# Selections over 136 candidate sums and one-pass weighted one-hot rows in a one-core decoder trunk

## The reference

```python
sc = jnp.einsum('bshcd,hcnd->bshcn', q, sub_keys)      # 8 heads, 2 halves, 128 keys each
top_s, top_i = lax.top_k(sc, 16)
cand_s = top_s[..., 0, :, None] + top_s[..., 1, None, :]             # 16 x 16 sums
cand_i = top_i[..., 0, :, None] * 128 + top_i[..., 1, None, :]
best_s, best_pos = lax.top_k(cand_s.reshape(..., 256), 16)
expert_idx = jnp.take_along_axis(cand_i, best_pos, axis=-1)
gates = jax.nn.softmax(best_s, axis=-1)
act = jax.nn.gelu(einsum('ced,cd->ce', expert_u[expert_idx], x))     # 128 experts a token
out = einsum('ce,ced->cd', gates * act, expert_v[expert_idx])
```

## Time and profile before

| what | us |
|---|---|
| runs: median of 3 (lowest to highest) | 2029.2 (2025.63 to 2031.04) |
| profiled execution: span from first to last instruction | 2043.0 |
| PE busy | 1942.4 |
| DVE busy | 1190.6 |
| POOL busy | 870.7 |
| ACT busy | 445.9 |

### The profile page before, as it was taken

The page is one execution under the profiler, slowest core; times in us unless marked ns, Lnnn a source line. Parts: engine busy times, 40 slices in busy tenths (PEclk is TensorE's granted clock), DMA queues, the critical chain, the costliest instruction groups (busy, mean ns, idle before and its releaser), DMA issues.

```text
span 2043.0 us, 23964 instructions
## 1 busy us (share of the span) xinstructions
PE 1942.4 (95%) x9007; PEld 1255.0 (61%) x9007; DVE 1190.6 (58%) x2972; ACT 445.9 (22%) x1045; POOL 870.7 (43%) x785
## 2 busy tenths in 40 slices
PE   8999999999889999999998888999999989999998
PEld 7688886956775887885676765444445543333332
DVE  1022101003896888788899989887867775444321
ACT  2233211111202454121211354000013321101112
POOL 0000000000684423445658355844557776666543
PEclk9999999999999999999999568999999999999999
DMA  7543454434999877999899677999999999999997
GB/s 237 147 121 109 148 155 144 145 103 136 373 388 349 280 255 239 369 386 388 331 359 371 221 261 243 410 409 409 409 376 348 344 334 410 409 409 409 409 389 278
DMA packets 252439, 613.48 MB, mean 300 GB/s; under 512 B 18676, under 2 KB 121124, under 8 KB 252324
## 3 DMA queue, kind: packets, MB, share of 16 engines
q0 software_dynamic: 110592, 402.70, 52.5%
q1 hardware_dynamic: 141120, 208.17, 29.7%
q10 hardware_dynamic: 612, 1.07, 0.2%
HBM read 609.77 MB, written 2.10 MB: 300 GB/s over the span
## 4 chain that ended last, share of the span: by engine, by line
PE 65%; DMA 13%; DVE 9%; POOL 7%; issue 3%; another core or an unknown queue 1%; ACT 1%; SPq 0%; POOLq 0%; DVEq 0%; ACTq 0%
PE ps L617 26%; PE ps L896 11%; PE ps L846 8%; DMA u_rows<-in_peer_u_dram,idx 7%; PE ps L632 7%; POOL u_rows L576 5%; DVE u_rows L1391 4%; PE ps L886 3%; PE ps L659 3%; POOL v_rows L590 2%; DMA wring<-in_w_in_dram 2%; DMA v_rows<-in_peer_v_dram,idx_turned 2%; PE ps L646 1%; PE ps L685 1%
## 5 line engine op out<-in xcount | busy, mean ns | idle before, releaser
L576 POOL DMA_INDIRECT u_rows<-in_peer_u_dram,idx x512 | 584.5, 1142 | 977.1 <-DVE idx L1378 508.2
L1391 DVE CUSTOM_DVE_ANT_0 u_rows<-u_rows,xn 128x1024 f32<-128x1024 f32 x512 | 621.3, 1217 | 177.8 <-DMA u_rows<-in_peer_u_dram,idx 165.2
L617 PE MATMUL ps<-xT,wring 128*128 128x256 f32 x2432 | 553.1, 386 | 22.3 <-DMA wring<-in_w_in_dram 10.1
L617 PEld LDWEIGHTS ps<-xT,wring 128*128 128x128 f32 x2432 | 464.0, 193 | 90.8 <-DMA wring<-in_w_in_dram 11.0
L896 PE MATMUL ps<-d_rows,gates 128*128 128x512 f32 x1024 | 456.3, 600 | 0.8 <-issue 0.8
L896 PEld LDWEIGHTS ps<-d_rows,gates 128*128 128x128 f32 x1024 | 190.7, 191 | 266.6 <-issue 266.6
L846 PE MATMUL ps<-v_rows,diag 64*64 64x512 f32 x1928 | 256.9, 633 | 18.9 <-DMA v_rows<-in_peer_v_dram,idx_turned 16.4
L590 POOL DMA_INDIRECT v_rows<-in_peer_v_dram,idx x121 | 135.4, 1119 | 131.3 <-PE ps L846 98.6
L886 PEld LDWEIGHTS ps<-hot_b,hot_a 128*128 128x128 f32 x1024 | 147.2, 230 | 55.4 <-issue 36.0
L886 PE MATMUL ps<-hot_b,hot_a 128*128 128x64 f32 x1024 | 155.0, 318 | 19.3 <-DVE hot_b L1458 11.0
L1091 ACT ACTIVATE diag<-ident,wgt 128x64 f32<-128x64 f32 x256 | 75.8, 336 | 435.6 <-PE ps L846 351.5
(11 more groups left out here) (201 smaller groups left out, 1747.0 us busy)
## 6 DMA issues: line engine op xcount, KB each, us to landing
wring<-in_w_in_dram SPq DMA_DIRECT2D x128, 512.0 KB
d_rows<-in_peer_v_dram SPq DMA_DIRECT2D x128, 512.0 KB
wring<-in_peer_w_query_dram SPq DMA_DIRECT2D x32, 512.0 KB
wring<-in_w_branch_conv_dram SPq DMA_DIRECT2D x16, 512.0 KB
wring<-in_w_branch_attn_dram SPq DMA_DIRECT2D x16, 512.0 KB
wring<-in_w_out_dram SPq DMA_DIRECT2D x16, 512.0 KB
wring<-in_xattn_wq_dram SPq DMA_DIRECT2D x16, 512.0 KB
wring<-in_xattn_wo_dram SPq DMA_DIRECT2D x16, 512.0 KB
```

The source lines that it names most:

```text
L576: pool.indirect_dma_start(out=u_rows[:, n % URING, :], out_offset=None, in_=peer_u[0], in_offset=bass.IndirectOffsetOnAxis(ap=experts_of(g ...
L617: mm = pe.matmul(bank(job)[:, 0:HN], w[:, k % 4, P * b:P * (b + 1)], act[:, k, :], start=(k == 0), stop=(k == KT - 1))
L1391: dve.tensor_tensor_reduce(out=u, in0=u, in1=(xn2 if h else xn1)[:, i, :], scale=1.0, scalar=0.0, op0=ALU.mult, op1=ALU.add, accum_out=dot ...
```

## The change

In `select`:

- `cand` holds 136 sums instead of 256: for each of the 16 first scores the sums with the 8 best second scores (positions 8a+b), then the first of the first scores with the other 8 second ones (positions 128 and up). The sums are sorted scores' sums, so the best 16 are always among these.
- Both indices are converted in one operation, the first no longer scaled by 128. `pos_ab` is split with other masks; `hot` is made for both numbers in one compare against two ramps `codes` (0 to 15, and 0 to 7 with 128 to 135) and one multiply. The scaling by 128 moves into the closing add.
- The generator yields twice less, so a selection ends one dot earlier.

In `one_hots` the compare and the multiply of `hot_b` over 8 tokens become eight `tensor_scalar` operations, one for each token, which compare a ramp of 64 with the token's expert number and multiply by its weight in one pass. Number and weight are one value per partition, read from `e2T` and `wT`. The semaphore `hot_half` is gone.

POOL makes one constant table more, so PE and DVE wait for 11 of them instead of 10, and the ramp `iota_a` counts in ones instead of in 128s.

```diff
-        cand = tiny("cand", [P, TOPK * TOPK])
+        cand = tiny("cand", [P, (TOPK + 1) * TOPK // 2])
...
-                candv = cand[:, :].rearrange("p (a b) -> p a b", a=TOPK)
-                t0 = after(dve.tensor_tensor(candv, top_v[:, 0, :].unsqueeze(2).to_broadcast([P, TOPK, TOPK]),
-                                             top_v[:, 1, :].unsqueeze(1).to_broadcast([P, TOPK, TOPK]), ALU.add))
+                near = TOPK // 2
+                pairs = cand[:, 0:TOPK * near]
+                rest_of_first = cand[:, TOPK * near:(TOPK + 1) * near]
+                sums = cand[:, 0:(TOPK + 1) * near]
+                dve.tensor_tensor(pairs.rearrange("p (a b) -> p a b", a=TOPK),
+                                  top_v[:, 0, :].unsqueeze(2).to_broadcast([P, TOPK, near]),
+                                  top_v[:, 1, 0:near].unsqueeze(1).to_broadcast([P, TOPK, near]), ALU.add)
+                t0 = after(dve.tensor_scalar(rest_of_first, top_v[:, 1, near:TOPK], top_v[:, 0, 0:1], None, ALU.add))
                 yield
-                dve.wait_ge(tk, t[0])
-                after(dve.tensor_scalar(top_f[:, 0, :], top_i[:, 0, :], float(NK), None, ALU.mult))
                 dve.wait_ge(tk, t0)
...
-                t2 = after(dve.tensor_copy(top_f[:, 1, :], top_i[:, 1, :]))
+                t2 = after(dve.tensor_copy(top_f[:, :, :], top_i[:, :, :]))
...
-                for c in range(2):
-                    t1 = after(dve.tensor_tensor(hot[:, c, :, :],
-                                                 pos_f[:, c, :].unsqueeze(2).to_broadcast([P, TOPK, TOPK]),
-                                                 iota16[:, :].unsqueeze(1).to_broadcast([P, TOPK, TOPK]),
-                                                 ALU.is_equal))
-                    yield
-                for c in range(2):
-                    dve.wait_ge(tk, t1 - 1 + c)
-                    after(dve.tensor_tensor(hot[:, c, :, :], hot[:, c, :, :],
-                                            top_f[:, c, :].unsqueeze(1).to_broadcast([P, TOPK, TOPK]), ALU.mult))
-                    yield
+                t1 = after(dve.tensor_tensor(hot[:, :, :, :],
+                                             pos_f[:, :, :].unsqueeze(3).to_broadcast([P, 2, TOPK, TOPK]),
+                                             codes[:, :, :].unsqueeze(2).to_broadcast([P, 2, TOPK, TOPK]),
+                                             ALU.is_equal))
+                yield
+                dve.wait_ge(tk, t1)
+                t1 = after(dve.tensor_tensor(hot[:, :, :, :], hot[:, :, :, :],
+                                             top_f[:, :, :].unsqueeze(2).to_broadcast([P, 2, TOPK, TOPK]), ALU.mult))
+                yield
...
-                dve.tensor_tensor(experts_of(g), to[:, 0, :], to[:, 1, :], ALU.add).then_inc(idx_rdy, 1)
+                dve.scalar_tensor_tensor(out=experts_of(g), in0=to[:, 0, :], scalar=float(NK), in1=to[:, 1, :],
+                                         op0=ALU.mult, op1=ALU.add).then_inc(idx_rdy, 1)
...
-                dve.tensor_tensor(hot_b[:, ch % 2, :, :],
-                                  e2T[:, i, o:o + 8].unsqueeze(2).to_broadcast([P, 8, 64]),
-                                  iota_b[:, 64 * hf:64 * (hf + 1)].unsqueeze(1).to_broadcast([P, 8, 64]),
-                                  ALU.is_equal).then_inc(hot_half, 1)
-                dve.wait_ge(hot_half, ch + 1)
-                dve.tensor_tensor(hot_b[:, ch % 2, :, :], hot_b[:, ch % 2, :, :],
-                                  wT[:, i, o:o + 8].unsqueeze(2).to_broadcast([P, 8, 64]),
-                                  ALU.mult).then_inc(hot_rdy, 1)
+                for t in range(8):
+                    last = dve.tensor_scalar(hot_b[:, ch % 2, t, :], iota_b[:, 64 * hf:64 * (hf + 1)],
+                                             e2T[:, i, o + t:o + t + 1], wT[:, i, o + t:o + t + 1],
+                                             ALU.is_equal, ALU.mult)
+                last.then_inc(hot_rdy, 1)
```

More of the change, by code:

```diff
@@ L313, in build_trunk @@
         eps_c = tiny("eps_c", [P, 1])
-        iota16 = tiny("iota16", [P, TOPK])
+        codes = tiny("codes", [P, 2, TOPK])
         xmax = tiny("xmax", [P, TT, XH])
@@ L398, in build_trunk @@
         t_out = sem("t_out")
-        hot_half = sem("hot_half")
         hot_rdy = sem("hot_rdy")
@@ L542, in _ @@
         def _(pool):
+            flat = hot[:, :, :, :].rearrange("p c a b -> p (c a b)")
             pool.memset(ident[:, :], 0.0).then_inc(consts, 1)
-            pool.memset(cand[:, 0:P], -1.0).then_inc(consts, 1)
-            pool.memset(cand[:, P:2 * P], 0.0).then_inc(consts, 1)
+            pool.memset(flat[:, 0:P], -1.0).then_inc(consts, 1)
+            pool.memset(flat[:, P:2 * P], 0.0).then_inc(consts, 1)
             pool.memset(eps_c[:, :], EPS).then_inc(consts, 1)
@@ L549, in _ @@
                                pattern=[[-1, P]], channel_multiplier=1).then_inc(consts, 1)
-            pool.affine_select(out=ntri[:, :], in_=cand[:, 0:P], compare_op=ALU.is_ge, fill=0.0, base=0,
+            pool.affine_select(out=ntri[:, :], in_=flat[:, 0:P], compare_op=ALU.is_ge, fill=0.0, base=0,
                                pattern=[[-1, P]], channel_multiplier=1).then_inc(consts, 1)
-            pool.affine_select(out=nmask_r[:, :], in_=cand[:, P:2 * P], compare_op=ALU.is_gt, fill=-1.0e30, base=0,
+            pool.affine_select(out=nmask_r[:, :], in_=flat[:, P:2 * P], compare_op=ALU.is_gt, fill=-1.0e30, base=0,
                                pattern=[[1, P]], channel_multiplier=-1).then_inc(consts, 1)
-            pool.tensor_copy(nones_r[:, :], cand[:, 0:P]).then_inc(consts, 1)
-            pool.iota(iota16[:, :], pattern=[[1, TOPK]], base=0, channel_multiplier=0,
+            pool.tensor_copy(nones_r[:, :], flat[:, 0:P]).then_inc(consts, 1)
+            pool.iota(codes[:, 0, :], pattern=[[1, TOPK]], base=0, channel_multiplier=0,
                       allow_small_or_imprecise_dtypes=True).then_inc(consts, 1)
+            pool.iota(codes[:, 1, :].rearrange("p (a b) -> p a b", a=2), pattern=[[P, 2], [1, TOPK // 2]], base=0,
+                      channel_multiplier=0, allow_small_or_imprecise_dtypes=True).then_inc(consts, 1)
             pool.wait_ge(consts, 5)
@@ L564, in _ @@
                               allow_small_or_imprecise_dtypes=True).then_inc(iotas, 1)
-                    pool.iota(iota_a[:, :], pattern=[[NK, NK]], base=0, channel_multiplier=0,
+                    pool.iota(iota_a[:, :], pattern=[[1, NK]], base=0, channel_multiplier=0,
                               allow_small_or_imprecise_dtypes=True).then_inc(iotas, 1)
@@ L597, in _ @@
         def _(pe):
-            pe.wait_ge(consts, 10)
+            pe.wait_ge(consts, 11)
             def transposes(job, tiles):
@@ L1336, in select @@
                     dve.wait_ge(gate_rdy, g - GRING + 1)
-                t1 = after(dve.max(best[:, r, 0:8], cand[:, :]))
+                t1 = after(dve.max(best[:, r, 0:8], sums))
                 yield
                 dve.wait_ge(tk, t[1])
-                t2 = after(dve.tensor_copy(top_f[:, 1, :], top_i[:, 1, :]))
+                t2 = after(dve.tensor_copy(top_f[:, :, :], top_i[:, :, :]))
                 dve.wait_ge(tk, t1)
-                t1 = after(dve.max_index(pos[:, 0:8], best[:, r, 0:8], cand[:, :]))
+                t1 = after(dve.max_index(pos[:, 0:8], best[:, r, 0:8], sums))
                 yield
                 dve.wait_ge(tk, t1)
-                t1 = after(dve.match_replace(cand[:, :], best[:, r, 0:8], cand[:, :], LOWEST))
+                t1 = after(dve.match_replace(sums, best[:, r, 0:8], sums, LOWEST))
                 yield
                 dve.wait_ge(tk, t1)
-                t1 = after(dve.max(best[:, r, 8:16], cand[:, :]))
+                t1 = after(dve.max(best[:, r, 8:16], sums))
                 yield
                 dve.wait_ge(tk, t1)
-                t1 = after(dve.max_index(pos[:, 8:16], best[:, r, 8:16], cand[:, :]))
+                t1 = after(dve.max_index(pos[:, 8:16], best[:, r, 8:16], sums))
                 dve.tensor_scalar(neg_best[:, r:r + 1], best[:, r, 0:1], -1.0, None, ALU.mult).then_inc(best_rdy, 1)
@@ L1354, in select @@
                 dve.wait_ge(tk, t1)
-                after(dve.tensor_scalar(pos_ab[:, 0, :], pos[:, :], 4, None, ALU.logical_shift_right))
-                t1 = after(dve.tensor_scalar(pos_ab[:, 1, :], pos[:, :], TOPK - 1, None, ALU.bitwise_and))
+                after(dve.tensor_scalar(pos_ab[:, 0, :], pos[:, :], 3, TOPK - 1, ALU.logical_shift_right,
+                                        ALU.bitwise_and))
+                t1 = after(dve.tensor_scalar(pos_ab[:, 1, :], pos[:, :], TOPK * near + near - 1, None,
+                                             ALU.bitwise_and))
                 yield
@@ L1489, in _ @@
                 dense_layers(unit)
-            dve.wait_ge(consts, 10)
+            dve.wait_ge(consts, 11)
             for g in range(2):
```

## The result

The change makes the kernel slower: 2039.88 us, median of 6 runs (2035.09 to 2046.23), against 2028.95 us (2023.14 to 2031.21) for the kernel before beside it. The ratio is 1.0058, with a 95% interval of 1.0038 to 1.0078. That is 11.8 us, 7.7 to 15.8. The forecast was 2025.1.

What follows compares the result with a forecast made beforehand. The prediction took DVE to lead the first gate build, with DMA or PE bounding most other stages. Terms -0.5 - 1.1 - 2.2 - 0.3 = -4.1 us took the median 2029.2 to 2025.1 us, range 2011 to 2045.

Steps and rivals of the forecast that it cites:

- rival 1: Gate builds: the second value is fetched after the first; +14.7 us in the first build, +15 overall, 2044 us; chance 0.28.
- I take the first: Gate build: two values fetched in the time of one, 161 ns an operation, 1.29 us for eight, 0.04 less than now.
- the term for the first build's chunks: First gate build: one-pass hot_b over 32 chunks changes DVE work by -1.3 us, with ends of -17 and +15.
- A microsecond of DVE is close to a microsecond of the program: First gate build, 1130 to 1268 us: DVE leads, busy 128.4 of 138 us, so its time counts nearly in full.
- the forecast's 0.8 for small savings: First gate build: 0.8 of the 2.8 us saved on DVE counts, since DVE also waits for PE: -2.2 us.
- A selection: Each of 32 selections takes 0.6 us less on DVE, mainly from maxima and index searches over 136 instead of 256 elements.
- Where it pays: Selection savings on the path: -0.5 us from 511 to 1037, -1.1 to 1130, part of the first build's -2.2, second build -0.3.
- The sum of -3.1 for the selections: Whole kernel: the selections' share of the predicted saving, -3.1 us, also used in the rivals' totals.
- The second build: Second gate build, 1504 to 1667 us: DVE has room, busy 128.0 of 163 us; predicted -0.3 us (0 to -1.2).
- The DMA-bound stages keep what a build gains or loses: Stages behind each gate build run at full DMA rate, so build gains or losses are not made up later; own term 0.
- Rival 4: First build: POOL's gathers hold DVE's short operations up to 0.9 us, some 10 times; +9 us, 2034 us; chance 0.06.
- Rival 2: Gate builds: one-pass operations run at single rate, one price for both values; +5.3 us, 2034 us; chance 0.10.

Runs made afterwards that it cites:

- experiment 8: The changed kernel with expert numbers and weights replaced by constants in both builds, so no value is read (timing only): ratio 0.9983 to the kernel before.
- Experiment 7: The changed kernel with weights replaced by the constant 1, so each operation reads one value (timing only): ratio 0.9980 to the kernel before.
- experiment 2: The kernel before with only the selections changed, hot_b still in two passes: ratio 0.9972 to the kernel before.
- experiment 10: Changed selections; hot_b from constants in the first build only, two passes in the second (timing only): 2029.77 us, ratio 0.9937 to the kernel before.
- experiment 9: The kernel before with only the selections changed, hot_b in two passes, run again in a later group: 2040.82 us, ratio 1.0003 to the kernel before.
- experiment 6: The kernel before with one-pass hot_b in the second build only, old selections: ratio 1.0005 to the kernel before.
- experiment 11: Changed selections; hot_b from constants in the second build only, two passes in the first (timing only): 2049.49 us, ratio 1.0038 to the kernel before.

## Why the prediction was wrong

What happened was rival 1: the second value costs as much again as the first, distances near 0.22 us, "and a first build of 150 us".

- **The step that failed** is "I take the first: the 63 ns look like the delay of a read, and two reads can share a delay". They don't: 0.102, 0.163 and 0.222 us with none, one and two values (experiments 8 and 7 and the change). Everything else in the price was right: 65 ns fixed, double rate, 63 ns for a value. The choice was between two ends that no row told apart, with 0.44 against 0.28, and the text's own argument against rival 1 was "nothing but the guess that reads overlap". Measured, the term for the first build's chunks is 32 x 0.45 = +14.4 us on DVE, where the sum had -1.3. Experiment 7, whose operations do cost the 0.16 us of the forecast, came out where the forecast did: 0.9980 is -4.1 us (-8.6 to +0.4), with a first build of 138.2. That the figure is met to the tenth is luck, but it shows that the other steps do not add up to an error of this size.
- **A microsecond of DVE is close to a microsecond of the program** in the first build: too much. Of 13.3 us more on DVE 9.7 came through, and 3.6 came out of its idle time, 1.6 of them recorded as waits for PE. Of 2.2 us less on DVE (experiment 2) nothing came through. Of 14.5 less (experiment 10 against 9) 8.5 came through in the build and 11 in the time. PE and DVE hand work to each other there through two places of `hot_a` and `hot_b`, so most likely neither leads alone; this was not tested apart. So rival 1's +14.7 at full price was too high, and the forecast's 0.8 for small savings as well.
- **A selection** was sized nearly right: -0.6 us each predicted, and over the whole program DVE is busy 1167.7 us in experiment 2 and 1190.6 before, which is -0.72 each. From dot 216 to 268, with three sums of selections, it is busy 2.3 us less. **Where it pays** was partly wrong. From 1037 to 1130 us I gave -1.1, because DMA is at 0.99 there; the stage became 2.5 us shorter in the mean of all traces (91.0 with the old selections, 88.5 with the new), its whole DVE saving. The first build was to give -1.2 and gave nothing. The sum of -3.1 for the selections lies within the intervals of both measurements (0.9972 and 1.0003).
- **The second build** was read rightly as having room: 15 us more of DVE's work cost 1 us there (experiment 6, -3 to +5). Rival 1's +3 lies in that interval too.
- **The DMA-bound stages keep what a build gains or loses**: right (experiment 10: 8.5 us gained in the build, 11 in the time).
- **Rival 4**, DVE held by POOL, is out for the change: see below. The evidence that the prediction had against it was none, though. It took half of L1199's 16 operations to run beside gathers; in the trace of the kernel before, eight of them stand before the first gather (511.1 us) and the other eight, 681 to 806 us, have no gather beside them either. **Rival 2**, single rate, is out too: 0.102 us with no value is near the 0.098 of double rate; single rate would make it 0.13.
- The measured +11.8 is thus some +9 from the first build, -2.5 from the stage before it, and a rest of some 5 us that the stages with noise of 10 us hide and that the interval (7.7 to 15.8) mostly allows.

## What to carry to other kernels

Splitting a broadcast operation into one operation per row trades elements for fixed prices: here 65 ns an operation and 60 ns for every value that it reads per partition, so a row must save more than that before one pass beats two. Count those prices from a measured operation with the same number of values, and where there is none, measure one before choosing between the ends. Put such a change to a test for each stage by itself, cut at program events rather than at times: one stage paid for it, the other didn't notice.

## What the runs showed of the hardware

- Values read per partition are paid one by one: 0.102, 0.163 and 0.222 us from start to start for 128x64 with none, one and two. The median durations of one operation, 189, 251 and 307 ns, lie as far apart; they are some 85 to 90 ns longer than the distances.

```profile
L1460 DVE TENSOR_SCALAR hot_b<-iota_b x512: 175/189/409, 1125.6 to 1661.2; 128x64 f32<-128x64 f32 x171
...
L1460 DVE TENSOR_SCALAR hot_b<-iota_b,e2T x512: 236/251/466, 1125.3 to 1656.0; 128x64 f32<-128x64 f32 x171
...
L1460 DVE TENSOR_SCALAR hot_b<-iota_b,e2T,wT x512: 296/307/567, 1122.7 to 1662.0; 128x64 f32<-128x64 f32 x171
```

- With two values, the operations of `hot_b` were not delayed by a gather of POOL beside them: of the 64 groups of eight, 54 ran beside a gather for at least 0.3 us, and 63 lasted 1.86 to 1.90 us, one 2.04. One place, both engines:

```profile
1157.41 1.88 DVE L1460 TENSOR_SCALAR hot_b<-iota_b,e2T,wT 128x64 f32<-128x64 f32 x8
...
1157.61 0.94 POOL L578 DMA_INDIRECT u_rows<-in_peer_u_dram,idx  x1 [3.73 <-DVE dots L1397]
```

  The Trainium skill, "SBUF — State Buffer", section "Who interferes with whom", says that DVE at double rate from memory contends with POOL: whichever starts first holds the ports they share for its whole instruction, and the other is blocked. Here, with two values, the two ran through each other without a visible delay on either; the trace doesn't agree.
- With no value the two do go slower together. In experiment 8 a group of eight lasts 0.90 us without a gather beside it, 0.94 in the median with one, and up to 1.15. POOL is busy 73.6 us in the first build of experiment 8 and 72.7 in that of experiment 10, and 64.3 to 68.2 in the other twelve traces, with 60 or 61 instructions in each. In the second build it is 138.6 (experiment 8) and 137.3 (experiment 11) against 125.1 to 134.8, although with fewer instructions. Why the values make the difference is open.
- With less DVE work in the second build the kernel became 8.7 us slower (experiment 11 against 9). In that build the chain of waits runs over POOL's gathers of `peer_v` for 44% of the time in experiment 11 and for 20% in experiment 9; in the other kernels that compute the gates in full it is from 5 to 32%, so the difference between two traces says little. Two explanations stand, neither tested: the slower gathers beside rows without values, or a DVE which is ready sooner and asks for its `peer_u` rows sooner, in front of the `peer_v` rows that PE waits for. The mechanism stays open.
